# Hybrid attention and SSD encoder: Q tiles made with the pairs, within-chunk SSD weights formed beside them, head loop rewritten

## The reference, cut to what matters

```python
proj = rmsnorm(x, pre_norm_g) @ w_in          # q, k, v, z_attn, z_ssm: 2048 columns each, xbc 3072, dt 64
o = dilated_attention(q, k, v, rel_bias_table)  # 16 heads x 128, banded, bias by distance
attn_out = rmsnorm(o) * silu(z_attn)
xbc = silu(conv(xbc) + conv_b)                # 5 taps
# SSD, both directions, 32 heads x 64, 4 groups, chunks of 128:
decay = exp(where(causal, a_cs[l] - a_cs[s], -inf))          # per head, chunk, direction
y_diag = einsum("bclsg,bclsgh,bcsghp->bclghp", C B^T, decay, x * dt)   # within chunks
y = y_diag + y_off + d_skip * xs                              # y_off: between chunks
ssm_out = rmsnorm(y * silu(z_ssm))
mix = concatenate([attn_out, ssm_out]) @ w_out
return x + rmsnorm(mix)
```

## Time and profile before

| | us |
|---|---|
| median of 3 runs (2438.7 to 2440.55) | 2439.43 |
| the profiled execution | 2437.86 |
| its span | 2436.1 |
| TensorE busy | 2405.7 (99%) |
| TensorE weight loads busy | 2284.2 (94%) |
| VectorE busy | 1731.5 (71%) |
| ScalarE busy | 979.3 (40%) |
| GpSimd busy | 389.5 (16%) |

### The profile page before, as it was taken

The page is one execution under the profiler, slowest core; times in us unless marked ns, Lnnn a source line. Parts: engine busy times, 40 slices in busy tenths (PEclk is TensorE's granted clock), DMA queues, the critical chain, the costliest instruction groups (busy, mean ns, idle before and its releaser), DMA issues.

```text
span 2436.1 us, 37150 instructions
## 1 busy us (share of the span) xinstructions
PE 2405.7 (99%) x13708; PEld 2284.2 (94%) x13708; DVE 1731.5 (71%) x2435; ACT 979.3 (40%) x1622; POOL 389.5 (16%) x580
## 2 busy tenths in 40 slices
PE   7999999999999999999999999999999999999998
PEld 6999999999999999999999999999999988888887
DVE  5686765555565555564787888788878768787767
ACT  6323433333333333333445444544454533234332
POOL 0000444444444444440000000000000000000000
PEclk9999999999999999999999999999999999999999
DMA  4235455555555555555464546554654435443544
GB/s 162 79 108 162 152 163 155 163 155 158 163 155 166 155 155 155 155 157 199 151 190 143 179 142 188 172 152 142 192 167 133 145 112 180 156 156 121 170 165 159
DMA packets 316776, 379.43 MB, mean 156 GB/s; under 512 B 20006, under 2 KB 237286, under 8 KB 313751
## 3 DMA queue, kind: packets, MB, share of 16 engines
q1 hardware_dynamic: 265063, 222.06, 29.9%
q10 hardware_dynamic: 33200, 106.02, 13.1%
q0 software_dynamic: 18432, 50.36, 6.6%
HBM read 299.16 MB, written 86.54 MB: 158 GB/s over the span
## 4 chain that ended last, share of the span: by engine, by line
PE 85%; DVE 1%; DMA 1%; ACT 1%; issue 0%; ACTq 0%; DVEq 0%; SPq 0%
PE ps L1012 35%; PE ps L810 22%; PE ps L1165 14%; PE ps L1085 4%; PE ps L971 2%; PE ps L938 2%; PE ps L905 2%; PE ps L921 1%; PE ps L981 1%; DMA w_raw<-in_w_in 1%; PE ps L945 0%; PE ps L912 0%; PE ps L954 0%; PE ps L994 0%; PE ps L1207 0%
## 5 line engine op out<-in xcount | busy, mean ns | idle before, releaser
L1012 PE MATMUL ps<-h_hi,w_hi 128*128 128x384 f32 x960 | 322.5, 336 | 0.0
L1012 PE MATMUL ps<-h_lo,w_hi 128*128 128x384 f32 x960 | 322.0, 335 | 0.0
L1012 PE MATMUL ps<-h_hi,w_lo 128*128 128x384 f32 x960 | 321.7, 335 | 0.0
L2194 DVE TENSOR_TENSOR w_lo<-raw_qk,w_hi 128x512 fp32r<-128x512 f32 x240 | 183.3, 764 | 182.7 <-ACT w_hi L1538 181.7
L810 PE MATMUL ps<-h_hi,w_hi 128*128 128x384 f32 x1056 | 275.1, 341 | 0.0
L1245 ACT ACTIVATE w_hi<-w_raw 128x512 fp32r<-128x512 f32 x176 | 109.9, 628 | 400.3 <-PE ps L810 271.2
L810 PE MATMUL ps<-h_lo,w_hi 128*128 128x384 f32 x1056 | 268.9, 335 | 0.0
L810 PE MATMUL ps<-h_hi,w_lo 128*128 128x384 f32 x1056 | 268.8, 335 | 0.0
L1012 PE MATMUL ps<-t_hi,w_hi 128*128 128x384 f32 x720 | 243.4, 338 | 0.9 <-DVE w_lo L2194 0.7
L1012 PE MATMUL ps<-t_hi,w_lo 128*128 128x384 f32 x720 | 243.5, 338 | 0.0
L1012 PE MATMUL ps<-t_lo,w_hi 128*128 128x384 f32 x720 | 242.6, 337 | 0.0
(11 more groups left out here) (327 smaller groups left out, 5183.9 us busy)
## 6 DMA issues: line engine op xcount, KB each, us to landing
raw_qk<-in_w_in SPq DMA_DIRECT2D x90, 512.0 KB, 4.3
w_raw<-in_w_in SPq DMA_DIRECT2D x176, 256.0 KB, 3.6
stage<-loc_scr ACTq DMA_DIRECT2D x16, 1536.0 KB, 7.3
stage<-t_scr SPq DMA_DIRECT2D x48, 512.0 KB, 3.6
stage<-in_w_out POOLq DMA_DIRECT2D x144, 128.0 KB, 2.8
t_scr<-stage POOLq DMA_DIRECT2D x144, 128.0 KB, 2.3
stage<-in_w_out SPq DMA_DIRECT2D x36, 512.0 KB, 3.7
stage<-zx_scr ACTq DMA_DIRECT2D x46, 384.0 KB, 8.9
```

Source lines behind the costliest of these rows:

```text
L1012: ins = nc.tensor.matmul(ps[:, bank, 0:HALF_T], w, h(k), start=(start and kk == 0 and q == 0), stop=(last and kk == KC - 1 and q == 2), sk ...
L2194: nc.vector.tensor_tensor(w_lo[:, n_slot(n, pp), :], src, w_hi[:, n_slot(n, pp), :].bitcast(f32), ALU.subtract).then_inc(w_lo_done, 1)
```

## The change

- **Pairs:** 38 in place of 30. Seven new pairs make Q tiles 1 to 14, one ("qz") makes Q's tile 15 with the attention gate of head 15. Direct tiles after the pairs go from 33 (Q and K of 16 heads, less Q's tile 0 which a pair makes, and the two gates of head 15) to 17 (K of 16 heads and the SSD gate of head 15).
- **Within-chunk weights:** 96 units, three in each of pairs 2 to 33, one per chunk and per tile of two heads. A unit: ScalarE's queue loads 256 KB of exponents, broadcast, into one buffer (`w_decay`) and 128 KB of C B^T; VectorE subtracts and takes the minimum (512 columns each); ScalarE takes exp into PSUM; VectorE multiplies (512) and adds (256); ScalarE's queue stores 128 KB to a DRAM scratch. `W_UNITS` gives for each unit the halves at which load, form, exp, sums and store stand. All three use the same buffer. `w_store` waits for the sums, and the next `w_load` and `half_hi` stand behind it.
- **Head loop:** written anew around the four chunks of K. Per iteration ScalarE's queue now also loads Q (384 KB) and the made weights (768 KB) in place of the 1.5 MB. `silu_of_xs(i)` waits until the stored y of head a has landed; TensorE's transposes of x, which now belong to head i and not to a, and the convolution for head i+1, wait for that SiLU. The SSD between chunks also belongs to head i. The scores of the next head wait for K's low part.
- **End:** four direct chunks in place of eight.

```diff
     0, 2048, 4096, 6144, 8192, 10240, 12288, 12800, 13312)
-LOOP_COLS = (COL_Q, COL_K)
-END_COLS = (COL_ZA + 15 * 128, COL_ZS + 15 * 128)
-Q, K = range(2)
-TILES = len(LOOP_COLS)
+END_COL = COL_ZS + 15 * 128
 PRO_TILES = 2 * SSM_GROUPS + 1
 PRO_CHUNKS = PRO_TILES * NCH
-IT_CHUNKS = TILES * NCH
+IT_CHUNKS = NCH
...
 XS_PAIRS = 8
 XS_P, Z_P = 1 + V_PAIRS, 1 + V_PAIRS + XS_PAIRS
-NP = Z_P + HEADS - 1
+Q_P = Z_P + HEADS - 1
+QZ_P = Q_P + (HEADS - 2) // 2
+NP = QZ_P + 1
 LAST_PP = (NP - 1) % 2
 FIRST_ORDER = (2, 3, 0, 1)
 PAIR_KINDS = {
@@ -73,6 +72,9 @@
     "xs": (2 * P, tuple(COL_XS + (n - 2 * XS_P) * P for n in range(2)),
...
     "z": (P, (COL_ZA - Z_P * P, COL_ZS - Z_P * P), ((ZX_ZA - Z_P) * P, (ZX_ZS - Z_P) * P)),
+    "q": (2 * P, tuple(COL_Q + (1 + n - 2 * Q_P) * P for n in range(2)),
+          tuple((ZX_Q + 1 + n - 2 * Q_P) * P for n in range(2))),
+    "qz": (0, (COL_Q + (HEADS - 1) * P, COL_ZA + (HEADS - 1) * P), ((ZX_Q + HEADS - 1) * P, (ZX_ZA + HEADS - 1) * P)),
 }
 CONV_TILES = PRO_TILES + WIN
 NC = CONV_TILES * NCH
@@ -95,6 +97,14 @@
     RUNS.append((_d, _lc, _src[0], len(_src), sum(r[3] for r in RUNS)))
 PAIRS = sum(r[3] for r in RUNS)
...
+W_FIRST = 2
+W_UNITS = ((0, 4, 4, 5, 6), (6, 7, 8, 9, 10), (10, 11, 12, 13, 13))
+W_PER = len(W_UNITS)
+OFF = 4 * P
@@ -167,7 +177,7 @@
...
+            def iteration(i, a):
+                order = FIRST_ORDER if a is None else range(NCH)
+                if a is not None:
+                    scores(a)
+                gemm_chunk(chunk_of(i, 0), tile_of(i), 0, order)
+                if a is not None:
+                    sample_scores(a)
+                    within_chunks(a)
+                gemm_chunk(chunk_of(i, 1), tile_of(i), 1, order)
+                if a is not None:
+                    transposed_probs(a)
+                else:
+                    pe.wait_ge(y12_back, 2)
+                    pe.wait_ge(c21_done, NP)
+                    pe.wait_ge(comb_done, 3 * NP)
+                gemm_chunk(chunk_of(i, 2), tile_of(i), 2, order)
+                transposed_x(i, a)
+                if a is not None:
+                    values(a)
+                else:
+                    pe.wait_ge(w_mat_done, W_PER * 2 * SSM_TILES)
+                transposed_v(i)
+                gemm_chunk(chunk_of(i, 3), tile_of(i), 3, order)
+                between_chunks(i)
...
-            def silu_of_xs(a):
-                act.wait_ge(conved, a + 1)
-                if a > 0:
-                    act.wait_ge(ys_stored, 16 * a)
+            def silu_of_xs(i):
+                act.wait_ge(conved, i + 1)
+                if i > 0:
+                    act.wait_ge(ys_stored, 16 * i)
                 silu(xsT, conv, xs_silu)
...
+            def q_hi_of(i):
+                act.wait_ge(q_in, 16 * i + 16)
+                nc.scalar.activation(q_hi[:, :], raw_qk[:, T:2 * T], ACT.Copy, scale=Q_SCALE).then_inc(q_hi_done, 1)
...
+            def w_load(a, group, c):
+                act.dma_start(w_decay.rearrange("p (d n) -> p d n", d=2),
+                              loc_scr.rearrange("(c d r) t -> c d (r t)", c=TT, d=2)[c][:, ds(a * (2 * P), 2 * P)]
+                              .partition_broadcast(P)).then_inc(decay_in, 16)
+                own = cb_scr[group * P:(group + 1) * P, PAIRS * P:].rearrange("p (d c n) -> p d c n", d=2, c=TT)
+                act.dma_start(w_own.rearrange("p (d n) -> p d n", d=2), own[:, :, c, :]).then_inc(own_in, 16)
+            def w_exp(a, c):
+                act.wait_ge(decay_arg, 2 * W_PER * a + (c + 1))
+                nc.scalar.activation(ps[:, 6, :], w_decay, ACT.Exp).then_inc(decay_exp, 1)
+            def w_store(a, c):
+                act.wait_ge(w_mat_done, 2 * W_PER * a + (c + 1))
+                act.dma_start(w_mat_scr[ds(a * P, P), :].rearrange("p (h c n) -> p h c n", h=2, c=TT)[:, :, c, :],
+                              w_made.rearrange("p (h n) -> p h n", h=2)).then_inc(w_stored, 16)
...
+                    if w is not None:
+                        a, group, c0 = w
+                        for q, (load, _, exp, _, store) in enumerate(W_UNITS):
+                            if n == store:
+                                w_store(a, c0 + q)
+                        for q, (load, _, exp, _, store) in enumerate(W_UNITS):
+                            if n == load:
+                                w_load(a, group, c0 + q)
+                            if n == exp:
+                                w_exp(a, c0 + q)
...
+            for group in range(SSM_GROUPS):
+                with act.Fori(W_FIRST // 2 + 4 * group, W_FIRST // 2 + 4 * group + 4) as g:
+                    pair(2 * g, 0, (g - W_FIRST // 2, group, 0))
+                    pair(2 * g + 1, 1, (g - W_FIRST // 2, group, W_PER))
+            with act.Fori(W_FIRST // 2 + SSM_TILES, NP // 2) as g:
                 pair(2 * g, 0)
                 pair(2 * g + 1, 1)
...
+            def iteration(i, a):
+                real = i < HEADS
+                nxt = lambda c: split_hi(chunk_of(i + 1, c), c, tile_of(i + 1))
                 if a is None:
-                    step(0, a, i, ip)
-                for s in range(NCH if a is None else 0, IT_CHUNKS):
-                    m = s + NCH
-                    split_hi(chunk_of(i, m), m % NCH, tile_of(i, m // NCH))
-                    step(s, a, i, ip)
-
-            iteration(0, 0, None)
-            for i in range(1, HEADS):
-                iteration(i, i % 2, i - 1)
+                    first_loads()
+                else:
+                    exps(a, 0)
+                    if real and i % 4 == 0:
+                        act.wait_ge(off_ready, i)
+                        load_cb(i // 4)
+                    if real:
+                        act.wait_ge(off_added, OFF_ADDED + a + 1)
+                        load_er(i)
+                if real:
+                    nxt(0)
+                if a is not None:
+                    if real:
+                        act.wait_ge(sscores_ready, a + 1)
+                        load_q(i)
+                    act.wait_ge(negmax, 2 * a + 2)
+                    if real:
+                        load_strip(i)
+                    exps(a, 1)
+                    if real:
+                        act.wait_ge(diag_ready, a + 1)
+                        load_w_mat(i)
+                if real:
+                    q_hi_of(i)
+                if a is not None:
+                    probs_out(a)
+                    if real:
+                        store_y(a)
+                    if i + 1 < HEADS:
+                        load_zx(zs, ZX_ZS, i, zs_in)
+                if real:
+                    silu_of_xs(i)
+                    if a is None:
+                        load_xs(1)
+                if a is not None:
+                    silu_of_za(a)
+                if i + 1 < HEADS:
+                    silu_of_zs(i)
+                if real:
+                    nxt(1)
+                    x_out(i)
+                else:
+                    for k in (1, 2):
+                        square_first(k)
+                    for k in range(GRP):
+                        first_m(k)
+                if a is not None:
+                    heads_out(a)
+                if real:
+                    v_out(i)
+                    if i + 1 < HEADS:
+                        load_zx(v_raw, ZX_V, i + 1, v_in)
+                    if i + 2 < HEADS:
+                        for part in range(2):
+                            make_strips(i // 2 * 2 + 2, 2 * (i % 2) + part)
+                    nxt(2)
+                    if i + 2 < HEADS:
+                        act.wait_ge(conved, i + 2)
+                        load_xs(i + 2)
+                    k_hi_of(i)
+                    if a is not None:
+                        store_att(a)
+                        load_zx(za, ZX_ZA, i, za_in)
+                    nc.scalar.activation(cur[0:1, 122:123], cur[0:1, 120:121], ACT.Exp)
+                    nxt(3)
...
+            def convolve_xs(i):
+                dve.wait_ge(xs_in, 32 * i + 32)
+                if i > 0:
+                    dve.wait_ge(xs_silu, i)
+                convolve(conv, xs_raw, lambda k: conv_cols[:, 24 * k + i:24 * k + i + 1], convb_cols[:, i:i + 1], conved)
+            def scaled_x(i):
+                dve.wait_ge(xt_out, 2 * i + 2)
+                if i > 0:
...
+            def w_form(a, c):
+                u = 2 * W_PER * a + c
+                d4 = w_decay.rearrange("p (r n) -> p r n", n=P)
+                col = loc4[:, ds(a, 1), :, c].rearrange("p q r -> p (q r)")
+                dve.wait_ge(decay_in, 16 * u + 16)
+                nc.vector.tensor_tensor(d4, d4, col.unsqueeze(2).broadcast_to([P, 4, P]), ALU.subtract).then_inc(decay_diff, 1)
+                dve.wait_ge(decay_diff, DECAY_DIFF + u + 1)
+                nc.vector.tensor_scalar(w_decay, w_decay, EXP_MAX, None, ALU.min).then_inc(decay_arg, 1)
+            def w_sum(a, c):
+                u = 2 * W_PER * a + c
```

(57 more changed lines are left out.)

859 lines of the change are left out of this document (376 added, 483 removed).

## The result

The changed kernel takes 2759.15 us (median of 4 runs, 2750.22 to 2763.09), the kernel before 2439.06 (4 runs): a ratio of 1.1306, 95% interval 1.1282 to 1.1330. The forecast was 2449, the range ended at 2490. The time is 310 us above the forecast.

What follows compares the result with a forecast made beforehand. TensorE was taken as the bound, busy almost throughout. Rest 256.9 and 421.3, pairs 1118.8, units 22.4, first iteration 24.3, loop 497.0, tail 104.8 gave 2445.5; plus 1.8 and 1.6, 2448.9 us; range 2405 to 2490.

Steps and rivals of the forecast that it cites:

- The gain on TensorE: Pairs and head loop: eight pairs replace 16 direct tiles, saving about 31.5 us; pair 29.44 us, iteration 31.8 us of TensorE.
- The units in the pairs: Pairs 2 to 33: the units' serial chain takes 30.1 us against TensorE's 29.4, costing 22.4 us in all.
- R2: Rival, pairs: broadcast loads land in 3.6 and 4.3 us, chain 31.7, total 2500 us; chance 0.11.
- The bounds: Units' load landings in the pairs: 2.8 us each at the low end, 3.6 and 4.3 at the upper.
- The walk: Once round the units' chain in a pair: 22.5 us and two landings, 28.8, plus 1.3 for longer VectorE operations.
- What the order costs: Pairs: with the units' chain at or below TensorE's 29.4 us per pair, the units cost nothing.
- The head loop: 15 iterations at 32.8 us plus about 5 for loads of C B^T: 497.0 us against 731.1.
- R3: Rival, head loop: y's store lands in 4.6 us, period 34.8, total 2479; in 9.8, 97 us more; chance 0.14.
- The forecast's own 32.8: Head loop: period of 32.8 us from one scores to the next, against TensorE's sum of 31.8.
- the cycle I named: Head loop: y's store lands, SiLU of x follows at 20.6 us, then TensorE's transposes and 12.1 to 12.2 us to scores.
- First iteration: First head iteration up to first scores: 22.4 us plus 1.9 of waiting for SiLU and scaled x, 24.3 against 22.9.
- Tail: After the last scores: three direct chunks and the between products leave, waits are added; 104.8 us against 120.6.

Runs made afterwards that it cites:

- e1: The changed kernel with the 96 units beside the pairs left out, the head loop loading other rows of the same size; 2474.97 us.
- e13: e12 with the one-element SiLU that loads the table moved ahead of the store of y, nothing left out; 2431.98 us, ratio 0.9964 to the kernel before.
- e3: The changed kernel with each unit's 256 KB loaded as 128 plain rows of another scratch instead of a broadcast, minimum 20; 2619.83 us.
- e4: The changed kernel with the subtraction writing PSUM and the next load of exponents issued early, behind the exp; 2551.64 us, ratio 1.0464.
- e6: The changed kernel with Q loaded first in the head loop, y stored before the probability copies, and er, strip and made weights loaded after them; 2751.24 us.
- e2: The changed kernel with all units kept but their load of exponents left out, weights from constants, work in PSUM; 2523.97 us.
- e7: The changed kernel with a one-element SiLU ahead of the wait for the store of y, so the table load runs before the landing; 2714.26 us.
- e9: The changed kernel with e4, e6, e7, two C B^T buffers and respaced units, zs loaded behind y's store, Q's parts late, first iteration reordered; 2476.21 us.
- e10: e9 with er, strip and made-weight loads issued behind the sample exps, most other issues behind the last weight chunk, zs's SiLU late; 2509.26 us.
- e11: e10 with strip, er and made weights issued between ScalarE's copies of x and of the heads; 2447.09 us, ratio 1.0024 to the kernel before.
- e12: e11 with the table load ahead of the probability copies and each pair's first C B^T issued two halves later; 2439.87 us, ratio 1.0001.

## Why the prediction was wrong

**The gain on TensorE** was right. e1's pairs take 29.33 us (forecast 29.44), e13's iterations 31.9 (floor 31.8). In e1 all 38 pairs go at the old pace.

**The units in the pairs** are the step that failed: "I take 2.9 for the first and, since raw blocks 0 and 1 are under way at the second, 3.4". The mechanism, a serial chain over one buffer that TensorE must follow, was right, and R2 named the long landings; their size was off, and so R2's price. With 5.9 twice the chain is 22.5 + 1.3 + 11.8 = 35.6 us; measured are (1401.9 - 6 x 29.3) / 32 = 38.3. The bounds came from rows of plain transfers. e3 shows that a plain load lands in 3.9 in this very place, inside the wider of the two bounds (4.3), and the broadcast of two rows in 5.9, outside them. A nearest row must be near in kind, not only in size. The page of the kernel before had two, among its DMA issues in the head loop, which I did not ask:

```profile
stage<-loc_scr ACTq DMA_DIRECT2D x16, 1536.0 KB, 7.3
stage<-er_scr ACTq DMA_DIRECT2D x32, 320.0 KB, 8.7
```

The first is the broadcast of the same exponents to 128 partitions, six times the size; the second is a broadcast too, but that first load stands ahead of it. Both are longer than the rows that I took for the units.

**A landing that the chain left out** is most of the missing 2.7 us. The walk has two landings per pair. The chain of waits has two that average 6.3 us, and in about every second pair a third, the raw block ahead of the next pair's first sum: 12.6 + 2.3 = 14.9 us per pair. The rest, 38.3 - 14.9 = 23.4, is what the walk gave for its other links, 23.8. The links of VectorE and ScalarE were sized well (form 0.72 + 0.49 us for 1.2). This is read from the chain; no run takes the raw block's landing away alone.

By the Trainium skill's page "DMA: Bandwidth & Descriptors", section "Anatomy of one DMA — SWDGE (gpsimd) path", 256 KB would land in 2.6 us, an estimate that the prediction put beside its own; the section is on transfers that GpSimd issues. The trace has 3.9 for plain rows and 5.9 for the broadcast, both on ScalarE's queue beside other transfers; the measurement decides.

**The clock** was no step of the prediction at all. In the pairs TensorE's busy time rose by 101 us against e1 (1213.9 and 1113.0, for the same matmuls) at a clock of 0.94. That this made the pairs longer is not shown, and the chain of waits speaks against it: TensorE has less than 3% of it, so slower matmuls filled time in which TensorE would have waited. Nor is the clock all of the 101 us: e4 has 27 us more than e1 (1139.6) at 1.00. In the loop TensorE is in the cycle, behind the SiLU, and there longer matmuls cost: its busy time is 495.3 us in the changed kernel at 0.97, and 488.6 in e6 and 480.7 in e13 at 1.00. So the clock has about half of these 15 us; the rest is open.

The Trainium skill's page "TensorE: Matmul & The Clock Gate", section "HAM oscillation — how this bites in real kernels", describes a loop that waits for a DMA in every round and runs on at the low clock after each wait, the loss coming on top of the wait. The trace agrees that the clock falls with such waits; that the loss comes on top it shows in the head loop alone.

**What the order costs** was set at nothing where the chain was shorter than a pair. e2 (no load of exponents, by my links 24 us) still takes 30.9 us per pair, e4 31.8. The units do not only form their own chain: ScalarE's stores and exps wait in the same order as the high parts, as e4's chain shows.

**The head loop** had the right cycle and the wrong landings: "Q has landed then" (7.1 us median, with er, strip and weights on the same queue), the store "lands 2.6 later" (4.3), and the SiLU at 1.3 with no table load behind the landing (1.28, e7). My R3 was this case at 34.8; 35.8 came: e13's 31.9, 2.8 of waiting and 1.0 of longer matmuls ((495.3 - 480.7) / 15), in part the clock's. R3's other price was off by my own terms: a landing of 9.8 for 2.6 is 7.2 us longer, not 6.5. The forecast's own 32.8 is what e11 and e12 show, but for another cycle, over VectorE from the SiLU to K's low part. The prediction gave VectorE the same 12.1 us, so the agreement is luck, and the prediction had said so: with the idle time ended by K's low part "the cycle I named is the wrong one, even at the right period".

**First iteration:** 1.9 us of waiting stood for two loads (5.9 and 8.5 us to landing) and two convolutions in a row. e9's order brings 26.9. **Tail:** 103.6 for 104.8, right.

The chances failed too. R2 and R3 were held to be alternatives with 0.11 and 0.14; both came. The range's upper end, 2490, left out R2 even at the price that I gave it, 2500.

## What to carry to other kernels

Before work is put beside a full engine, write down which transfers stand *in* its chain, and price each by a row of the same kind and under the load that the change itself makes; what depends on a landing is to be issued as soon as its buffer is read, not when its turn comes. Where TensorE is in the cycle, a long wait can cost more than its length, by the clock; where it only follows a longer chain, its slower matmuls are no loss to count. And when loads are reordered, follow the next transfer on the same queue: e4, e6 and e10 moved one landing out of the cycle and put another one in.
